# A mixer's work order on TensorE, VectorE and ScalarE rewritten, one step at a time

## What is computed

```
proj = x @ w_in
c_q, c_kv, k_pe, pr = split(proj)
q   = rms_norm(c_q) @ w_uq ; ckv = rms_norm(c_kv) ; rotary on q_pe and k_pe
u   = pr + mu * (prev(pr) - pr)            # token shift
r, k, v, w_lo, a_lo, g_lo = split(u)
decay = exp(-exp(-softplus(-(w0 + tanh(w_lo) @ w2)) - 0.5))
a = sigmoid(a0 + a_lo @ a2) ; g = sigmoid(g_lo) @ g2
kk = k * k_k, normed per head
s_t = s_{t-1} * decay + (s_{t-1} (-kk)) (kk*a)^T + v kh^T ; y_t = s_t r_t
y = (group_norm(y) + bonus) * g
```

## Time and profile before

| | us |
|---|---|
| three runs, median (lowest, highest) | 3268.62 (3267.70, 3272.02) |
| the profiled execution, its own time | 3262.0 |
| its span, first to last instruction | 3259.1 |
| turns 2 to 16 of the mixer, from one `y_centred` to the next, 15 periods | 1168.39 (77.9 each) |
| turns 17 and 18 (without stage a), to the end of the mixer | about 89 |
| stages after the mixer | about 1859 |

### The profile page before, as it was taken

The page is one execution under the profiler, slowest core; times in us unless marked ns, Lnnn a source line. Parts: engine busy times, 40 slices in busy tenths (PEclk is TensorE's granted clock), DMA queues, the critical chain, the costliest instruction groups (busy, mean ns, idle before and its releaser), DMA issues. The chain is left out here.

```text
span 3259.1 us, 66235 instructions
## 1 busy us (share of the span) xinstructions
PE 2919.8 (90%) x26600; PEld 2220.4 (68%) x26600; DVE 1740.4 (53%) x3820; ACT 967.0 (30%) x2497; POOL 587.6 (18%) x875
## 2 busy tenths in 40 slices
PE   7999999999999999669898998899957999989990
PEld 6888888888888888545555555555535776666770
DVE  1666666666666666558686868622253222222225
ACT  2333333333333333234443444312211111111115
POOL 0001000000000000010000000011104645555650
PEclk9999999999999999689999999999968999999995
DMA  6111121211111112420101010034318899776546
GB/s 192 35 38 36 37 40 37 39 37 36 37 37 36 38 37 40 93 86 1 38 1 39 1 35 1 34 117 129 129 52 304 257 371 291 241 228 164 104 95 245
DMA packets 337227, 310.23 MB, mean 95 GB/s; under 512 B 235201, under 2 KB 290529, under 8 KB 322529
## 3 DMA queue, kind: packets, MB, share of 16 engines
q1 hardware_dynamic: 315424, 238.88, 24.1%
q0 software_dynamic: 21504, 67.13, 9.2%
HBM read 208.12 MB, written 84.42 MB: 90 GB/s over the span
## 5 line engine op out<-in xcount | busy, mean ns | idle before, releaser
L802 PE MATMUL mx_bank<-mx_xT,mx_w_in 128*128 128x128 f32 x5168 | 647.6, 282 | 17.3 <-DVEq L286 13.8
L802 PEld LDWEIGHTS mx_bank<-mx_xT,mx_w_in 128*128 128x128 f32 x5168 | 606.3, 195 | 83.3 <-issue 60.6
L1485 PE MATMUL at_bank<-pl_kT,pl_qT 128*128 128x512 f32 (+5 forms) x656 | 291.1, 530 | 2.3 <-issue 2.3
L1457 ACT ACTIVATE at_PQ<-at_bank,at_nms 128x512 f32<-128x512 f32 (+5 forms) x328 | 192.7, 596 | 253.6 <-DVE at_nms L1585 252.1
L2276 PE MATMUL ex_down<-ex_wd,ex_hT 128*128 x512 | 236.4, 605 | 26.9 <-ACT ex_hT L2205 25.4
L2153 POOL DMA_INDIRECT ex_x<-scr_hx,ex_idx x256 | 247.0, 965 | 68.1 <-issue 60.1
L2252 PE MATMUL ex_gate<-ex_wg,ex_xT 128*128 x1024 | 234.1, 382 | 17.5 <-SPq L2125 17.5
L2252 PEld LDWEIGHTS ex_gate<-ex_wg,ex_xT 128*128 128x128 f32 x1024 | 196.3, 192 | 71.3 <-issue 47.3
L2212 ACT ACTIVATE ex_y<-ex_down,ex_gcol 128x512 f32<-128x512 f32 x128 | 81.0, 683 | 525.4 <-POOL ex_gcol L2160 186.1
L2252 PE MATMUL ex_up<-ex_wu,ex_xT 128*128 x1024 | 231.6, 379 | 0.0
L1628 DVE COPY at_PT<-at_bank 128x512 f32<-128x512 f32 (+3 forms) x328 | 196.3, 600 | 45.7 <-PE at_bank L1497 28.0
(11 more groups left out here) (315 smaller groups left out, 4681.3 us busy)
## 6 DMA issues: line engine op xcount, KB each, us to landing
ex_wg<-in_w_eg SPq DMA_DIRECT2D x32, 1024.0 KB
ex_wu<-in_w_eu SPq DMA_DIRECT2D x32, 1024.0 KB
ex_wd<-in_w_ed SPq DMA_DIRECT2D x32, 1024.0 KB
mx_x<-in_x SPq DMA_DIRECT2D x76, 128.0 KB, 3.8
pl_ro_x<-in_x SPq DMA_DIRECT2D x17, 512.0 KB, 4.3
scr_hx<-ro_h SPq DMA_DIRECT2D x17, 512.0 KB, 2.6
scr_acc<-ro_ha SPq DMA_DIRECT2D x17, 512.0 KB, 3.1
co_r<-scr_acc SPq DMA_DIRECT2D x17, 512.0 KB, 5.6
```

The lines of the kernel that those rows point to most:

```text
L802: ins = pe.matmul(dst, w_in[:, k, col:col + n], xT[:, k, :], start=(k == 0), stop=(k == KC - 1))
L1457: ins = a.activation(PQ[:, n % NP, 0:full], b[:, 0:full], ACT.Exp, bias=bias, scale=SCALE, accum_out=sums[:, j, h, 1 + gi:2 + gi])
L1485: t.mark(pe.matmul(bank[n % SB][:, 0:wd], qT[h][keys(h), j * P:(j + 1) * P], kT[h][keys(h), k0 * P:k0 * P + wd], start=True, stop=True), f ...
```

## The change

Four module constants are given. No other line is touched; every step does what it did.

```
-PE_ORDER = ("aacaabcaaaaaaabaaabaaaaaaaaaaaaaaabababbbaabaaababbbabababab"
-            "abababaababbbabbbb")
-ACT_ORDER = "bbbcbbcbbbaabbbbbaacaaaabbbabbb"
-VEC_ORDER = "bcbbbbbcbabbbbbcabbbbbcbbbbbbbbbbbabbabababbbbbabaab"
+PE_ORDER = ("acaaabacaaabaaabaaaaaaaaaaaaaaaabbbbaabaabaaababbbababababab"
+            "aaabaabaababbbbbbb")
+ACT_ORDER = "bbbcbbbcbabbabbababcaaaabbabbbb"
+VEC_ORDER = "cbbbbbbbbcabbbbcbbabbbbcbbbbbbbbbababababbabbbbbbaab"
+SP_ORDER = "bcbbaabaabaacaab"
 SP_ORDER = "bbcaabbbacaaaaab"
```

## The result

The changed kernel took 3235.74 us (median of 4 runs, 3231.33 to 3241.36) against 3270.32 for the kernel before (4 runs, 3267.70 to 3272.50): ratio 0.9896, 95% interval 0.9878 to 0.9913, 1.0% faster. The direction was forecast; the size was not. The forecast was 3259.6, and the lower end of the range 3249.0.

A forecast was written before the change was run, and what follows sets the result against it. TensorE was taken to bound the kernel, busy 90% of the span. Terms -9.0 (15 periods), +0.3, -1.9 and +1.6 gave -9.0 us: 3253.0 on the profiled execution, 3259.6 on the median; range 3249 to 3277.

The forecast's parts named there:

- The bound: Mixer: TensorE, busy 96% in turns 2 to 16; only its waits and the low clock, about 54 us, can be won.
- The list of waits: TensorE, each turn: `kpe_sum` and `rms_sums` waits go; `lora_w` 0.43, `kk_norm` 1.8, `SA1` 0.49 come; `state_add1` 0.48 stays.
- `g_lo` 0.54 later: ScalarE, head of the turn: `g_lo` and its table load wait for the later `u_low`, starting 0.54 us later.
- the 0.43 of `lora_w`: TensorE, head of the turn: a new wait of 0.43 us for the later end of `g_lo`.
- Rival 3: ScalarE, head: the table load of `g_lo` runs under its wait, giving -18 us, 3250; chance 0.10.
- `kk_norm` 1.8: TensorE, head of the turn: a new wait of 1.8 us for `kk_sq` of ScalarE.
- the overlap of two ACTIVATEs that I took away at `w_tanh`: ScalarE, head: the table switch now between `w_tanh` and `a_tanh` loses 0.12 us of overlap, delaying `kk_sq`.
- TensorE's own time: Each turn: 19 pieces of stage a instead of 20 save about 0.2 us, 74.31 becoming 74.1.
- The low clock: TensorE, turns 2 to 16: 1.6 us a stretch; with one wait of 1.8, one stretch left in 15 turns.
- Rival 1: TensorE: the low clock comes in nearly every full turn behind the 1.8 wait, +12 us, 3280; chance 0.15.
- The tail and turn 1: Outside the 15 periods: turn 1 costs +0.3 us; turn 17 gains 1.9 through an earlier `s_init`.
- The rule on the clock: TensorE: by the skill page idleness brings the low clock, leaving no 1.6 us to win; the forecast followed the trace instead.

The follow-up runs named there:

- e7: Changed kernel with the two waits ahead of `g_lo` written in the other order, so its table load waits for `u_low`: 3245.5 us, 0.9944 of the kernel before.
- e6: Changed kernel with `ckv_sq`, `kpe_part` earlier on ScalarE, `cum`, `mid`, `sq_sum` ahead of `y_rs` on VectorE, `kk_norm` behind `rms_sums` on TensorE: 3224.9 us.
- e9: e6 with TensorE's `lora_g` between `ckv_proj` and `kpe_sum`, and `kk_norm` three steps behind `rms_sums` instead of two: 3217.2 us, 0.9862 of the kernel before.
- e10: e9 with the last steps of qp put back as in the kernel before and `sq_sum` ahead of `cum` on VectorE: 3214.2 us, 0.9860 of the kernel before.
- e5: Changed kernel with `kk_sq` behind `ckv_sq` and `kpe_part` on ScalarE: 3246.3 us, 0.9942 of the kernel before.
- e8: Changed kernel with two more ACTIVATEs a turn ahead of `kk_sq` on ScalarE, into a buffer nobody reads: 3267.8 us, 1.0024 of the kernel before.
- e3: Changed kernel with VectorE's order of before put back: 3238.0 us, 0.9919 of the kernel before.

## Why the prediction was wrong, point by point

**The bound: right.** The mixer's 15 periods are TensorE's time, its waits and the low clock, and nothing else moved in them.

**The list of waits: right but for one.** `kpe_sum` and `rms_sums` lost theirs, `kk_norm` and `SA1` got theirs, no wait came in the middle. `SA1` measured 0.48 for 0.49.

**`g_lo` 0.54 later: wrong, the step that failed first.** "Its table load with it: the load of line 760 began behind its wait" was carried from the earlier trace rows to another instruction. The load ran under the wait. In the sum this is the 0.43 of `lora_w`, 6.5 us in 15 turns. Rival 3 had the mechanism, and was given 0.10 for the sake of that row. Its price was 3250, which is still 14 us above the 3235.7 measured.

**`kk_norm` 1.8: measured 1.34**, 6.9 us in 15 turns. About 0.35 of the 0.46 would have been off even with the late load, as e7 shows with 1.45. Without the late load the working puts TensorE at `kk_norm` 14.36 us into the turn and the end of `kk_sq` at 15.98; measured are 14.55 and 15.84. Most of the second difference is the overlap of two ACTIVATEs that I took away at `w_tanh`: it came back where `w_tanh` now follows `u_own_v` (1138.24 + 2.43 - 1140.58 = 0.09). Why TensorE came 0.19 later isn't known.

**TensorE's own time: mis-sized.** 74.31 became 73.78, not 74.1: 4.8 us. The count of pieces by which I sized it carries only a part. One period each of e6, e9 and e10:

```profile
827.00:902.58 75.58, 73.97 (x1088) 66.69 (x1086) 49.91 (x91) 26.00 (x61) 5.19 (x4) 1.00 0.21 40
821.00:895.87 74.87, 73.90 (x1089) 66.70 (x1088) 49.58 (x92) 25.82 (x62) 5.20 (x4) 1.00 0.20 40
818.61:893.27 74.66, 74.18 (x1087) 66.89 (x1088) 49.53 (x92) 25.90 (x61) 5.19 (x4) 1.00 0.21 39
```

e10 has one piece more than e9 (20 for 19) and takes 0.28 more a turn, near the 0.2 of the prediction. But the changed kernel, e6 and e9 all have 19 pieces, counted in their texts (the expectation of e9 took it for one fewer), and take 73.78, 73.97 and 73.90. Which neighbours cost the time is open; it was not tried.

**The low clock: the price right, the condition wrong.** 1.6 a stretch was reckoned, 1.58 measured. That 1.8 in one piece would leave one stretch is refuted: at 1.77 e5 has six. That the forecast escaped this error was luck: the wait turned out to be 1.34. The two rows of before, 2.01 without and 2.11 with, said how two waits with matmuls between them had done in two turns, and I read a limit for one wait into them. Other turns of the same trace already spoke against a limit at 2.1: turn 5 waited 1.46 and 0.61, 2.07, and has a stretch. Rival 1 (12 us slower) would have been nearly right for its 1.8 to 2.1, as e8 shows.

**The tail and turn 1.** Turn 17: -2.4 for -1.9. `y_centred` of turn 2 is 0.8 later, for 0.3, with one stretch of low clock in turn 1 that had none before.

Together: the 15 periods were forecast at 1161.1 (15 x 77.3 + 1.6) and took 1141.1; 6.5 + 6.9 + 4.8 and the 1.6 are 19.8 of the 20.0. Between the profiled executions the miss is 17.3 (3253.0 for 3235.7), mostly since the stages behind the mixer, left out of the sum, were 3.7 longer. On the median it is 23.9: the forecast added the 6.6 by which the runs of the kernel before lay above its profiled execution, and those of the changed kernel lay around its own.

**The rule on the clock.** "TensorE: Matmul & The Clock Gate" in the Trainium skill (Part 1) has the low clock come back after a whole window in which the engine is idle. The trace differs from it still: in e8 TensorE is never idle for more than about 2.12 us at a time in these turns, it is busy for 96% of them, and 14 of the 15 have a stretch.

**The range** had its lower end where rival 3 ended. All terms on one side, each of 5 to 7 us in 15 turns, were taken as if they would not add up.

## What to carry to other kernels

Where an engine is busy for 96% and its clock falls after waits, added waiting can cost more than its length: 0.42 us more cost 1.06 a turn, and 0.78 cost 2.26. Count the stretches of low clock beside the waits, and shorten first the waits that they follow. Here those were the waits at the head of the turn; the two of 0.48 at its end never had one behind them. Look up which of several waits each instruction of the built kernel carries, table loads among them, before a delay is passed on through it. And before one wait is taken away, compute when the next condition behind it is met: here it took two engines' orders together, and with either put back the gain was gone.

## What the runs showed of the hardware that I had not expected

A table load does not always wait with its ACTIVATE: at 1135.87 it ran while `u_low` was still computed, and with the two waits exchanged it idled 0.72 us for it. The number of low-clock stretches rises from 0 of 15 turns at a wait of 1.34 or 1.45 to 6 at 1.77 and 14 at 2.12, at the same work. Yet the length of the wait alone isn't the condition: one turn of e3 has a stretch behind 1.33 and 0.20, and one of e8 has none behind 2.12. And without such stretches the turns are even: fourteen periods within 0.02 us. That the whole run is steadier for it is not shown: 17 runs of the kernel before spread over 17.6 us and six of the changed one over 10.4, but ten of e8, with a stretch in nearly every turn, over 8.3.
